# Picking three experts from the first token tile's counts, with the router's scratch moved and two tiles' affine on GpSimd

## What is computed

```
x = post_norm(i, 0, x, g1, out)                      # out: attention times w_o
x = channel_mixer(i, x, sh2, sc2, g2)

def hier_moe(h, w_rg, b_rg, w_re, b_re, w_gate, w_up, w_down):
    g_logits = xt @ w_rg + b_rg                      # 4 groups
    g_sel = argmax(g_logits)                         # top-1 group
    e_in_group = (xt @ w_re + b_re)[group g_sel]     # 8 experts in it
    top_v, top_i = top_k(e_in_group, 2)              # top-2 experts
    gates = softmax(top_v) * softmax(g_logits)[g_sel]
    # for every expert e with tokens, in any order:
    #   hb = silu(xb @ w_gate[e]) * (xb @ w_up[e]);  y[tok] += (hb @ w_down[e]) * w
```

## Time and profile before

| what | value |
|---|---|
| median of 3 runs | 1338.85 us (1335.91 to 1342.24) |
| the profiled execution | 1335.58 us, span 1333.8 us |
| PE busy | 1131.6 us (85%) |
| DVE, ACT, POOL busy | 471.6, 151.7, 162.4 us |
| moved by DMA | 377.78 MB, mean 283 GB/s |

### The profile page before, as it was taken

The page is one execution under the profiler, slowest core; times in us unless marked ns, Lnnn a source line. Parts: engine busy times, 40 slices in busy tenths (PEclk is TensorE's granted clock), DMA queues, the critical chain, the costliest instruction groups (busy, mean ns, idle before and its releaser), DMA issues.

```text
span 1333.8 us, 29278 instructions
## 1 busy us (share of the span) xinstructions
PE 1131.6 (85%) x11200; PEld 602.5 (45%) x11201; DVE 471.6 (35%) x1222; ACT 151.7 (11%) x402; POOL 162.4 (12%) x316
## 2 busy tenths in 40 slices
PE   4899998779889999777765999887967989999863
PEld 1333335445455656433333444444444555555431
DVE  0120206767733333222116002277675323333215
ACT  0110115600000000000002000345000000000000
POOL 3000001210211111111001110000011211111100
PEclk9899998989689999889877999979977999999977
DMA  9876785024998999999996994200239999997993
GB/s 365 311 283 231 303 350 222 1 63 163 379 411 329 414 415 414 415 415 414 415 374 227 118 144 159 80 0 1 79 131 415 412 415 372 415 414 286 414 416 145
DMA packets 79835, 377.78 MB, mean 283 GB/s; under 512 B 14920, under 2 KB 15376, under 8 KB 52136
## 3 DMA queue, kind: packets, MB, share of 16 engines
q1 hardware_dynamic: 61504, 343.48, 65.7%
q0 software_dynamic: 12208, 30.95, 8.6%
q10 hardware_dynamic: 6072, 2.69, 0.7%
HBM read 373.91 MB, written 7.87 MB: 286 GB/s over the span
## 4 chain that ended last, share of the span: by engine, by line
PE 40%; DMA 38%; issue 10%; DVE 6%; ACT 3%; DVEq 1%; POOLq 1%; SPq 1%; POOL 0%; ACTq 0%; PEldq 0%
DMA ring<-in_w_down_dram 36%; PE ps L803 16%; PE ps L956 6%; PE ps L1093 6%; PE ps L1106 4%; PE ps L1076 3%; DMA ring<-in_w_ada_dram 2%; PE ps L779 1%; PE ps L901 1%; POOLq L467 1%; PE ps L889 1%; PE ps L923 1%; DVEq L1143 1%; ACT hT L690 1%; ACT hT L703 1%
## 5 line engine op out<-in xcount | busy, mean ns | idle before, releaser
L1093 PE MATMUL ps<-ring,xs 128*32 128x256 f32 x4672 | 299.9, 411 | 75.1 <-DMA ring<-in_w_up_dram 68.4
L803 PE MATMUL ps<-ring,hT 128*128 128x512 f32 x576 | 254.8, 602 | 9.5 <-ACT hT L637 4.2
L1093 PEld LDWEIGHTS ps<-ring,xs 128*32 128x32 f32 x4672 | 164.5, 117 | 198.4 <-issue 116.2
L803 PEld LDWEIGHTS ps<-ring,hT 128*128 128x128 f32 x576 | 109.6, 192 | 153.6 <-issue 142.0
L1106 PE MATMUL ps<-ring,hm 128*32 128x256 f32 x2336 | 143.7, 382 | 7.8 <-DMA ring<-in_w_down_dram 7.8
L1617 DVE TENSOR_TENSOR hp<-sg,ps 128x128 f32<-128x128 f32 x73 | 21.0, 287 | 304.2 <-ACT sg L741 304.2
L1076 PE MATMUL ps<-yo,place 32*128 32x256 f32 x1800 | 119.9, 394 | 2.4 <-DVE place L1625 2.4
L1624 DVE TENSOR_TENSOR yo<-ps,gt 128x512 f32<-128x512 f32 x73 | 50.5, 691 | 142.9 <-PE ps L1106 142.9
L1076 PEld LDWEIGHTS ps<-yo,place 32*128 32x128 f32 x1800 | 80.2, 185 | 44.5 <-issue 31.6
L1106 PEld LDWEIGHTS ps<-ring,hm 128*32 128x32 f32 x2336 | 67.2, 109 | 73.4 <-DVE hm L1618 18.9
L741 ACT ACTIVATE sg<-ps 128x128 f32<-128x128 f32 x73 | 20.2, 277 | 596.6 <-PE ps L1093 596.6
(11 more groups left out here) (297 smaller groups left out, 825.7 us busy)
## 6 DMA issues: line engine op xcount, KB each, us to landing
ring<-in_w_gate_dram SPq DMA_DIRECT2D x82, 1024.0 KB, 15.0
ring<-in_w_up_dram SPq DMA_DIRECT2D x82, 1024.0 KB, 15.4
ring<-in_w_down_dram SPq DMA_DIRECT2D x82, 1024.0 KB, 15.5
ring<-in_w_ada_dram SPq DMA_DIRECT2D x48, 1024.0 KB, 8.0
ring<-in_w_qkv_a_dram SPq DMA_DIRECT2D x12, 1024.0 KB, 5.4
ring<-in_w_qkv_b_dram SPq DMA_DIRECT2D x12, 1024.0 KB, 14.6
ring<-in_w_o_a_dram SPq DMA_DIRECT2D x4, 1024.0 KB, 10.0
modb<-mdram POOLq DMA_DIRECT2D x8, 512.0 KB, 10.7
```

What stands on the lines that cost most here:

```text
L803: ins = mm(ps[:, 2 * t + hf, :], lhs[:, k, t * P:(t + 1) * P], raw[:, slot, kk * D + hf * 512:kk * D + (hf + 1) * 512], start=(k == 0), st ...
L1093: ins = mm(ps[j * BLK:(j + 1) * BLK, 6, 0:W].rearrange("p (a f n) -> p a f n", a=2, f=G), xs[:, k, :], w[:, :, kk * DE:(kk + 1) * DE].rear ...
```

## The change

Six things are changed. (1) The picks are now three, and they come from tile 0's logits: each token's first choice is counted by a matmul over the 128 tokens, and the three experts with the fewest choices, but at least one, are taken (`early_picks`), right after tile 1 is normalised. logits(0) stand in the middle of wo_tile(2). (2) `rt` lies in modb[0:2], the modulation rows of tile 0, which are used up after tile 0; larger parts of it lie in the small region (`late`, `where`). (3) The third expert's load no longer waits for the router; it waits for logits(2), for xmod and for the affine of tiles 0 and 1. (4) That affine is done by GpSimd, three operations per tile. (5) In layer 0, two of the eight chunks of the sixth modulation are loaded ahead of w_o and their waves are done ahead of the transpose of tile 2 of the attention's output; the other six waves stand two behind the count and four behind logits(2). (6) A picked expert counts as having at least one block, and the three picks are ordered by their place.

```
-        rt = kT[:, :, :].rearrange("p k n -> p (k n)")
+        rt = modb[:, 0:2, :].rearrange("p a d -> p (a d)")
...
-        WO0 = [QKV_A + 12 + 4 * KD]
+        WO0 = [QKV_A + 12 + 4 * KD + 2]
...
-        ADA_BANK = (6, 6, 7, 6, 7, 1)
+        ADA_BANK = (6, 6, 7, 6, 7, 6)
...
                 sp.wait_ge(sel_rdy, l + 1)
-                picks = [table(sp, T_PRE + i, 0, NE - 1) for i in range(2)]
+                picks = [table(sp, T_PRE + i, 0, NE - 1) for i in range(BUFS)]
                 sp.wait_ge(out_done, 32 * (l + 1))
                 for i in range(2):
                     load(i, picks[i], BASE[i], None)
+                sp.wait_ge(xmod_w[l], 16 * NT)
+                sp.wait_ge(rt_pe[l], 1)
+                sp.wait_ge(x01_rdy, 2 * (l + 1))
+                load(2, picks[2], BASE[2], None)
...
-                sp.wait_ge(xmod_w[l], 16 * NT)
-                sp.wait_ge(rt_free, l + 1)
-                load(2, table(sp, T_LIST + 2, 0, NE - 1), BASE[2], None)
...
                     pool.dma_start(xmod[t * P:(t + 1) * P, :], o[:, t, :]).then_inc(xmod_w[l], 16)
+                    if t < NT - 1:
+                        chain(pool.tensor_scalar(x[:, t, :], x[:, t, :], mv[:, t, 0:1], rstd[:, 4 + t:5 + t], ALU.subtract, ALU.mult))
+                        chain(pool.tensor_tensor(x[:, t, :], x[:, t, :], lnb[:, 2, :], ALU.mult))
+                        chain(pool.tensor_tensor(x[:, t, :], x[:, t, :], lnb[:, 3, :], ALU.add))
+                        pool.sem_inc(x01_rdy, 1)
...
+                    transpose_tiles(lambda t: o[:, t, :], o_rdy[l], oT_ps[l], tiles=range(2))
+                    pe.wait_ge(o_ev[l], 5)
+                    ada_wave(5, 0)
+                    ada_wave(5, 1)
+                    transpose_tiles(lambda t: o[:, t, :], o_rdy[l], oT_ps[l], tiles=(2,))
...
+                        if t == NT - 1 and c == WO_N // 2:
+                            logits(0).then_inc(lg_rdy, 1)
...
                 turn_x(1)
-                logits(0).then_inc(lg_rdy, 1)
                 logits(1)
...
-                waves(0, 2)
+                pe.wait_ge(top_rdy, l + 1)
+                mm(ps[0:1, 7, P:P + NE], ones[:, 0:1], rt[:, 384:384 + NE], start=True, stop=True).then_inc(top_ps, 1)
+                waves(2, 4)
                 turn_x(2)
                 logits(2).then_inc(rt_pe[l], 1)
-                waves(2, 6)
+                waves(4, 8)
...
+            def early_picks(l):
+                dve.wait_ge(lg_rdy, l + 1)
+                chain(v.tensor_tensor(lg0, ps[:, 0, 0:NG + NE], br[:, l, :], ALU.add))
...
+                v.tensor_scalar(rt[:, 384:384 + NE], lg0[:, NG:], best, None, ALU.is_ge).then_inc(top_rdy, 1)
+                dve.wait_ge(top_ps, l + 1)
+                top = ps[0:1, 7, P:P + NE]
+                v.tensor_scalar(far, top, 0.0, 8192.0, ALU.is_equal, ALU.mult)
+                chain(v.scalar_tensor_tensor(key, top, float(NE), cst[0:1, C_IOTA:C_IOTA + NE], ALU.mult, ALU.add))
+                chain(v.tensor_tensor(key, key, far, ALU.add))
+                for i in range(BUFS):
+                    chain(v.tensor_reduce(least[:, i:i + 1], key, AX, ALU.min))
+                    if i < BUFS - 1:
+                        chain(v.tensor_scalar(far, key, least[:, i:i + 1], 32768.0, ALU.is_equal, ALU.mult))
+                        chain(v.tensor_tensor(key, key, far, ALU.add))
...
+                v.tensor_single_scalar(tabi[:, T_PRE:T_PRE + BUFS], lead, NE - 1, op=ALU.bitwise_and).then_inc(sel_rdy, 1)
...
-                    if t < NT - 1:
-                        chain(centre_rows(t, lnb))
-                        chain(spread_rows(t, lnb))
+                    if t == 1:
+                        early_picks(l)
...
+                chain(v.tensor_scalar(rt[0:NE, 602:603], rt[0:NE, 1436:1437], -LEAD / 4, None, ALU.is_lt))
+                chain(v.tensor_scalar(rt[0:NE, 600:602], rt[0:NE, 600:602], rt[0:NE, 602:603], None, ALU.max))
```

More of the change, by code:

```diff
@@ L292, in ada_chunk @@
                 return qkv_chunk(0, 8 + a // 4) + 1 + a % 4
[L293 removed]
+            return WO0[0] - 2 + k if k < 2 else ADA1 + k - 2
         def waves_of(c):
@@ L362, in _ @@
                             load_ada(i, k)
+                if l == 0:
+                    for k in range(2):
+                        load_ada(5, k)
                 wo = w_o[l].rearrange("a (k p) n -> p (a k) n" if l else "a (p k) n -> p (a k) n", k=KD)
@@ L370, in _ @@
                 if l == 0:
-                    for k in range(KD):
+                    for k in range(2, KD):
                         load_ada(5, k)
@@ L378, in load @@
                         if freed is None:
-                            last = MOE0[l] - 1 - (MOE0[l] - 1 - s) % RING if i == 1 else MOE0[l] - 1 - (KD if l == 0 else 0)
+                            last = MOE0[l] - 1 - (MOE0[l] - 1 - s) % RING if i == 1 else WO0[l] + WO_N - 1
                             sp.wait_ge(st_free, RING + last + 1)
@@ L998, in waves @@
                             ada_wave(5, a)
-                waves(0, 2)
+                wo_tile(0)
+                wo_tile(1)
+                turn_x(0)
+                if l == 0:
+                    pe.wait_ge(ld_wr, 16 * LAYERS * 4)
+                wo_tile(2)
+                turn_x(1)
+                logits(1)
+                pe.wait_ge(top_rdy, l + 1)
+                mm(ps[0:1, 7, P:P + NE], ones[:, 0:1], rt[:, 384:384 + NE], start=True, stop=True).then_inc(top_ps, 1)
+                waves(2, 4)
                 turn_x(2)
                 logits(2).then_inc(rt_pe[l], 1)
-                waves(2, 6)
+                waves(4, 8)
                 pe.wait_ge(rt_dve[l], 1)
@@ L1537, in _ @@
                 for i in range(2 * NT):
-                    v.tensor_scalar(col(2400 + i * P, P), cst[:, C_POS:C_POS + P], sf[:, 6 + i:7 + i], None, ALU.is_equal)
-                    v.tensor_scalar(col(3200 + i * NBX, NBX), iota[:, 0:NBX], sf[:, i:i + 1],
+                    v.tensor_scalar(where[:, i * P:(i + 1) * P], cst[:, C_POS:C_POS + P], sf[:, 6 + i:7 + i], None, ALU.is_equal)
+                    v.tensor_scalar(col(1706 + i * NBX, NBX), iota[:, 0:NBX], sf[:, i:i + 1],
                                     rowf[:, i:i + 1], ALU.is_equal, ALU.mult).then_inc(rt_dve[l], 1)
-                a_slot = col(3200, 2 * NT * NBX).rearrange("p (i n) -> p i n", n=NBX)
+                a_slot = col(1706, 2 * NT * NBX).rearrange("p (i n) -> p i n", n=NBX)
                 dve.wait_ge(rt_pe[l], 5)
-                val, empty, half, tok = (rt[:, 3600 + i * NBX:3600 + (i + 1) * NBX] for i in range(4))
+                val, empty, half, tok = (late[:, i * NBX:(i + 1) * NBX] for i in range(4))
                 chain(v.tensor_scalar(val, ps[:, 7, 64:64 + NBX], -1.0, None, ALU.add))
@@ L1553, in _ @@
                                        ALU.is_gt, ALU.mult).then_inc(rt_dve[l], 1)
-                count, third, rest, spare, more, turned = (one_row(a, 1) for a in range(2045, 2051))
-                di = one_row(2044, 1).bitcast(I32)
-                dummies, cum, paired, tail = (one_row(a, N_CUM) for a in (1500, 1600, 1640, 1680))
+                count, third, rest, spare, more, turned = (one_row(a, 1) for a in range(1235, 1241))
+                di = one_row(1234, 1).bitcast(I32)
+                dummies, cum, paired, tail = (one_row(a, N_CUM) for a in (1500, 1600, 1640, 1540))
                 chain(v.tensor_scalar(count, ps[0:1, 6, 256:257], float(LEAST), None, ALU.max))
```

99 lines of the change are left out of this document (42 added, 57 removed).

## The result

The changed kernel takes 1327.31 us (median of 7 runs, 1326.32 to 1331.46) against 1337.9 us before (7 runs, 1334.3 to 1342.24): a ratio of 0.9929, 95% interval 0.9913 to 0.9945. Timed a second time it is 0.9925 (0.9911 to 0.9939). By these two ratios the change takes 9.5 to 10 us off (10.6 between the first pair of medians). The forecast was 18.3 off, 1320.5.

What follows compares the result with a forecast made beforehand. Both mixtures were taken as a race of expert loads (15.55 us) against TensorE blocks (6.84) through three buffers. 9.3 (layer 0) plus 9.0 (layer 1) gave 18.3 off, 1317.3 profiled, 1320.5 as median; forecast 1312 to 1328, range up to 1334.

Steps and rivals of the forecast that it cites:

- hole at 410:421: Layer 0: DMA idle while the fifth load waits for expert 19's buffer; most of 7.0 us of idle time to go.
- five loads behind the long wait: Layer 1: expert 30 becomes 12th, so five loads instead of six follow its buffer, taking 79.7 us against 95.1.
- The third rival: Layer 1 keeps six loads behind expert 30, giving 1336, or first loads start no earlier; 13%.
- The earlier start: Layer 0: earlier picks send the first expert load out at 337.7, 4.9 us earlier.
- the megabyte moved behind the first load: Layer 0: xmod and gate pieces, 1 MB that used to move ahead of the first load, cost 2.6 us.
- 30 ends at 1226.1 and its first slots are free at 1221.5: Layer 1: when expert 30's blocks end and its buffer frees, against 1215.00 before; five loads then end at 1301.2.
- the recurrence: Count of loads against blocks through three buffers; on the old order within 2 us in layer 0, 0.2 in layer 1.
- (1): Rival: GpSimd and VectorE block each other during tile 1's normalisation and the picks; slower, 1349 at slip 17; 10%.
- An operation above 3.7: Sign of being wrong upward: a GpSimd operation longer than 3.7 us, where whole overlap would use up the gain.
- The standstill ahead of the counts: Sign: VectorE idle for 9 us between the early picks' first operations and the counting matmul's result.
- (2): Rival: small handover waits start the first block 6 to 10 us later than counted; 1327 to 1335; 15%.
- a possible 2.8 of clock in wo_tile(0) of layer 0: Layer 0: waves moved into idle time might keep the clock up, 30.61 against 27.8 us; not counted in the sum.

Runs made afterwards that it cites:

- the later load: Changed kernel, but in layer 1 only the first load also waits until tile 2's rows are stored: 1336.62 us, ratio 0.9988.
- 25 third: Changed kernel, but in layer 1 the three picks are overwritten by the constants 18, 27 and 25: 1323.25 us, ratio 0.9887.
- its removal: Changed kernel, but the affine of tiles 0 and 1 is back on VectorE, behind each tile's normalisation: 1324.49 us, ratio 0.9888.

## Why the prediction came out as it did

**Right.** The direction, and the mechanism in both layers; the size was not. The two mixtures gave 8.9 of the 18.3 forecast, and it is partly luck that the time still came out at 1327.3, just inside the 1312 to 1328 given to the forecast: 2.5 us came from the attention of layer 1, for which nothing was forecast. Layer 0: first load at 337.56 (forecast 337.7), tile 2 done at 344.3 (344.8), first block at 380.70 (381.5), no hole at 410:421. Layer 1: first block 98.9 after wo_tile(0) (98.0), and five loads behind the long wait instead of six. Those are worth what the sum said: from expert 30's buffer to the landing of the last w_up it was 90.2 (1305.22 - 1215.00) and is 74.9 (1295.77 - 1220.84), 15.3 less (15.4 in the second profiles). The third rival did not happen.

**Wrong in size, layer 0: 9.3 forecast, 6.0 measured.** The earlier start gave 5.2 (56.3 against 61.5 after wo_tile(0)), the hole its 7.0 and the megabyte moved behind the first load its 2.6, as forecast (neither is measured apart from the DMA share of 1.01 where the hole was). Two terms were missing. The first 17 us of loads ran at 350 GB/s instead of 389, which is 17.4 x 39 / 410 = 1.7 us; the last w_up landed 7.1 earlier than before (407.2 and 406.9 against 414.0 and 414.3 after wo_tile(0)), where the four terms leave 7.9. And the last block of the layer, which TensorE did at the full clock before, now ran at half of it (granted clock 1.00 in 695.2:697 before, 0.50 in 688.5:692 now). Before:

```profile
695.18 1.93 PE L1093 MATMUL ps<-ring,xs 128*32 128x256 f32 x32 [1.70 <-DMA ring<-in_w_up_dram]
...
700.04 1.07 PE L1106 MATMUL ps<-ring,hm 128*32 128x256 f32 x16 [0.41 <-DMA ring<-in_w_down_dram]
```

and changed:

```profile
688.47 3.64 PE L1109 MATMUL ps<-ring,xs 128*32 128x256 f32 x32 [1.36 <-DMA ring<-in_w_up_dram]
693.64 1.93 PE L1122 MATMUL ps<-ring,hm 128*32 128x256 f32 x32
```

From the start of the last half to the end it was 5.9 us and is 7.1: 1.2 us (6.0 and 6.9 in the second profiles). The change is not shown to be its cause. In layer 0 two kernels built on the changed one, with the later load and with 25 third, have 1.93 there; in layer 1 both the kernel before and the changed one have 1.93 in one of their two profiles and 3.64 in the other. That makes 1.2 to 1.3 of the 2.9 and 2.5 by which these mixtures scatter.

**Wrong in size, layer 1: 9.0 forecast, 2.8 measured.** The failed step is "30 ends at 1226.1 and its first slots are free at 1221.5", 287.9 after wo_tile(0). Measured: 295.3, and 293.9 in the second profile. Of the 7.4 in the first, 1.6 are the first load, 55.2 instead of 53.6 (the lock of GpSimd, shown by its removal). 3.4 came before expert 21: its second pair of transfers landed 101.6 after the first load, where the recurrence had 98.2 (103.4 for all six slots less two at 2.6). The low rate makes 20 x 35 / 410 = 1.7 of that; the rest I can't place. 2.4 came behind it: after the wait of 3.45 TensorE did the half block in 3.64 and the adding in 2.67, instead of 1.93 and 1.59, which is 2.8; the granted clock of 1080:1090 was 0.66 (in the second profile only 0.9 came behind it). The recurrence had no clock in it but a fixed 1.8 at the start.

What made the three terms weigh fully is what the experiments show: where the first block starts in the changed kernel, the chain of layer 1 runs through the load of 21 and not through that block; 5.2 us later it has begun to run through both. Putting 21 sixth instead of fifth bought one load fewer behind 30 (15.3) and paid 13.9 for it ahead of 30 (11.2 in the second profiles, 12.5 in the mean), of which the forecast had only 6.5.

**The rivals.** (1) was the wrong price for a real thing: GpSimd's operations took 3.80, 2.35 and 2.35, 8.5 for a tile and not 7.5, and in layer 1 VectorE stood behind three of them for 2 us each; 2.1 of it lay on the path, in layer 0 none. It cost some 5 us by the ratios and 3 by the medians, while I had given it 10% as a loss of more than the gain. An operation above 3.7 was named as a sign of that loss and did appear (3.80); it did no such harm because VectorE stood for three of the six operations of the layer only, and for most of that in time it had to spare. The standstill ahead of the counts, forecast at 9 us, was 4.20 in layer 1 and 6.48 in layer 0. (2), the first block later still, was not it (98.9 against 98.0), and by the experiments 5 us of it would have cost between nothing and 2.5 in layer 1.

**Not forecast:** 2.5 us in the attention of layer 1, at a granted clock of 0.94 instead of 0.92. Both values occur in kernels of the changed family, so the change is not shown to be its cause. I had left out a possible 2.8 of clock in wo_tile(0) of layer 0; there 30.61 became 30.09.

## What to carry to other kernels

Where loads and blocks race through a few buffers, move one end at a time before believing a sum: the first load 12 us later cost 9 us here, the first block 5 us later at most 2.5, and that only where its slack ended. A big expert late in the list saves a load behind it only as far as nothing new waits ahead of it; here it paid to keep big ones apart (4 to 5 us for an expert of 4 blocks taken from the 11th place to the 3rd, and one of 3 put back for it, tried once). And work moved to GpSimd is not beside VectorE just because nobody waits for it: look for small VectorE operations that last as long as a GpSimd one.

## What the runs showed of the hardware

- A small VectorE tensor_tensor (one element per partition, or 32 in one) took 2.15 to 2.28 us instead of 0.16 to 0.18 while GpSimd did a tensor_tensor of 128x1024, to the end of it; one of GpSimd's took 3.15 instead of 2.36 when it began during a VectorE operation with two SBUF tensors; a 128x1024 operation with two SBUF tensors beside GpSimd's tensor_scalar took its usual 1.23.
- GpSimd took 3.80 us for a tensor_scalar of 128x1024 with two per-partition scalars, more than the 2.35 of a tensor_tensor of that size. The Trainium skill (GPSIMD Engine Reference, 3.1) has 4497 ns for a tensor_tensor of 2048, which halved is 2.25 as an estimate; the trace has 2.35.
- The last half block of layer 1, after a wait of 1.4 to 1.9 us, ran in 1.93 us in one execution and in 3.64 in another of the same kernel.
- While tile 2's store and the gate pieces ran beside them, the first expert loads moved 350 to 358 GB/s with a DMA share of 0.94 to 0.97, against 389 before; which of the small transfers does it was not tried apart, except that the affine rows are not it, and that loads which waited for tile 2's store moved 379.
